# Attention's second pass: the masks come from ScalarE and VectorE copies instead of TensorE products

## The reference

```python
DILATED_PATTERNS = ((128, 1), (512, 4), (2048, 16))
def _dilated_pattern(qh, kh, vh, window, dilation):
    ...
    s = jnp.einsum('brnikge,brnjke->brnkgij', qs, kk)
    delta = ATTN_BLOCK + qi - kj
    band = (delta >= 0) & (delta <= steps)
    s = jnp.where(mask[:, None, None], s, -jnp.inf)
    m = jnp.max(s, axis=-1)
    pexp = jnp.exp(s - m[..., None])
    l = jnp.sum(pexp, axis=-1)
    o = jnp.einsum('brnkgij,brnjke->brnikge', pexp, vv)
```

## Time and profile before

| | |
|---|---|
| median of 3 runs | 3047.01 us |
| lowest, highest | 3043.47, 3048.12 us |
| profiled execution, span | 3041.8 us |
| profiled execution, its own device time | not given apart from the span |
| mixers phase in the trace | about 690 to 1223 us |
| second passes in the trace | 775.3 to 868.5, 913.7 to 1005.4, 1043.7 to 1223.0 us |

### The profile page before, as it was taken

One profiled execution on the slowest core, in us unless ns is written; L12 is line 12 of the kernel. 1 busy time (PEld: TensorE's weight loads), 2 busy tenths in 40 slices (PEclk: granted clock), 3 DMA queues, 4 the chain that ended last, 5 costly groups with the idle time before them and its releaser, 6 DMA issues. The chain is left out here.

```text
span 3041.8 us, 38698 instructions
## 1 busy us (share of the span) xinstructions
PE 2929.7 (96%) x14818; PEld 2301.9 (76%) x14818; DVE 1999.7 (66%) x2492; ACT 1147.6 (38%) x1734; POOL 284.0 (9%) x278
## 2 busy tenths in 40 slices
PE   7999999997999999899999999899999999999999
PEld 5678887884657566688778888788888788877887
DVE  7334555117575755545698899889998786776743
ACT  5332121212434344311255544554444444444321
POOL 0000000003435443000001000000000000000000
PEclk9999999998999999999999999999999999999999
DMA  4452222237775764634322234525542666443632
GB/s 145 166 190 64 62 83 62 74 84 194 200 186 152 203 154 136 199 124 142 140 104 83 97 122 159 197 84 194 194 152 104 243 210 222 149 158 114 192 113 67
DMA packets 260088, 435.02 MB, mean 143 GB/s; under 512 B 44013, under 2 KB 128493, under 8 KB 252877
## 3 DMA queue, kind: packets, MB, share of 16 engines
q1 hardware_dynamic: 255534, 408.32, 42.8%
q0 software_dynamic: 4384, 24.41, 2.2%
HBM read 312.18 MB, written 120.00 MB: 142 GB/s over the span
## 5 line engine op out<-in xcount | busy, mean ns | idle before, releaser
L103 PE MATMUL up_banks<-up_x_hi,up_w_hi 128*128 128x512 f32 x1232 | 484.0, 393 | 23.4 <-DVE up_x_lo L2682 8.2
L104 PE MATMUL up_banks<-up_x_lo,up_w_hi 128*128 128x512 f32 x1232 | 482.0, 391 | 0.0
L105 PE MATMUL up_banks<-up_x_hi,up_w_lo 128*128 128x512 f32 x1232 | 481.8, 391 | 0.0
L103 PE MATMUL inp_ps<-inp_h_hi,carry_q 128*128 128x512 f32 x896 | 353.1, 394 | 15.1 <-DVE inp_h_lo L202 9.7
L105 PE MATMUL inp_ps<-inp_h_hi,carry_k_two 128*128 128x512 f32 x896 | 349.8, 390 | 0.0
L104 PE MATMUL inp_ps<-inp_h_lo,carry_q 128*128 128x512 f32 x896 | 349.7, 390 | 0.0
L103 PEld LDWEIGHTS up_banks<-up_x_hi,up_w_hi 128*128 128x128 f32 x1232 | 232.8, 189 | 78.9 <-issue 15.7
L105 PEld LDWEIGHTS up_banks<-up_x_hi,up_w_lo 128*128 128x128 f32 x1232 | 232.8, 189 | 48.5
L104 PEld LDWEIGHTS up_banks<-up_x_lo,up_w_hi 128*128 128x128 f32 x1232 | 233.0, 189 | 48.2 <-issue 0.2
L2723 DVE SCALAR_TENSOR_TENSOR carry_rows<-carry_squares,up_conv_w,carry_rows 128x1024 f32<-128x1024 f32 x176 | 232.2, 1319 | 24.4 <-ACT carry_rows L2554 19.4
L103 PE MATMUL down_banks<-down_x_hi,down_w_hi 128*128 128x512 f32 x616 | 240.6, 391 | 7.1 <-DVE down_x_lo L2194 7.1
(11 more groups left out here) (378 smaller groups left out, 5366.2 us busy)
## 6 DMA issues: line engine op xcount, KB each, us to landing
carry_room<-in_w_up_dram SPq DMA_DIRECT2D x84, 512.0 KB, 4.4
act<-carry_rows SPq DMA_DIRECT2D x44, 512.0 KB, 2.9
carry_room<-cum_rows SPq DMA_DIRECT2D x16, 1024.0 KB, 6.6
carry_room<-x SPq DMA_DIRECT2D x7, 2048.0 KB, 9.4
carry_room<-in_w_in_dram SPq DMA_DIRECT2D x26, 512.0 KB, 5.9
xbc<-carry_room SPq DMA_DIRECT2D x12, 1024.0 KB, 5.7
carry_room<-xbc SPq DMA_DIRECT2D x16, 768.0 KB, 4.4
down_x<-act SPq DMA_DIRECT2D x12, 1024.0 KB, 7.2
```

The source lines that it names most:

```text
L103: pe.matmul(out, w_hi, x_hi, start=first, stop=False, skip_group_check=onto)
L104: pe.matmul(out, w_hi, x_lo, start=False, stop=False, skip_group_check=onto)
L105: return pe.matmul(out, w_lo, x_hi, start=False, stop=last, skip_group_check=onto)
```

## The change

Steps 0 and 1 of each second pass stay. For steps 2 to 39 the mask product is gone. ACT copies the mask of step k + 2 into the bank right after the exponential of an even step k (`lay_mask`, in `scalar`); DVE copies the masks of odd steps in a generator of its own (`lay_odd_masks`), due at k - 1.35. Both wait for the exponential of step g - 2. PE waits for the copy (`laid`) instead of the exponential, and all its products of that step run with start=False onto what the copy has left. 19 steps of each group are ACT's, 19 are DVE's: 76 copies for each engine. The pace changes too: a second pass is 69.0 long instead of 75.0, and a chunk of the scan comes every 23.1 instead of 24.5.

```diff
--- before.py
+++ after.py
@@ -788,6 +788,7 @@
          self.den_in, self.den_add, self.den_inv, self.inv_st) = (
             ph.sem(f"a_{n}") for n in ("built ones neg_in mm max m_mm m_out m_in m_s m_neg s_mm exp pv_mm "
                                        "o_add o_st den_in den_add den_inv inv_st").split())
+        self.laid = [ph.sem(f"a_laid_{engine}") for engine in ("act", "dve")]
         self.first_in = [ph.sem(f"a_first_in{n}") for n in range(2)]
         self.half_in, self.cleared = ph.sem("a_half_in"), ph.sem("a_cleared")
         self.k_in, self.k_last_in, self.q_in = ([ph.sem(f"a_{name}_in{n}") for n in range(len(self.SPANS))]
@@ -839,6 +840,31 @@
         if k < 2 * TT:
             return 1, k - TT, k % 4 < 3
         return 2, 2 * (k - 2 * TT), False
+
+    LAID = (STEPS - 2) // 2
+
+    def own_mask(self, g, k):
+
+        bank = self.banks[:, g % 2].rearrange("p (h b t) -> p h b t", h=2, b=2)
+        p, col, follows = self.step(k)
+        if p == 2:
+            return self.banks[:, g % 2], self.up_k[:, :, :].rearrange("p u t -> p (u t)")
+        if p == 1:
+            blocks = 2 if follows else 1
+            return bank[:, :, 0:blocks], self.both_k[:, :, 0:blocks]
+        if follows:
+            return (bank.rearrange("p h b t -> p h (b t)").rearrange("p h (i x) -> p h i x", i=RES),
+                    self.near_k[:, :, :, :, :].rearrange("p h i b m -> p h i (b m)"))
+        return bank[:, :, 0].rearrange("p h (i x) -> p h i x", i=RES), self.near_k[:, :, :, 0]
+
+    def lay_mask(self, engine, r, k):
+
+        g = r * self.STEPS + k
+        out, mask = self.own_mask(g, k)
+        if g == 2:
+            engine.wait_ge(self.built, 13)
+        engine.wait_ge(self.exp_s, g - 1)
+        return out, mask
 
     def readers(self, g):
 
@@ -1013,6 +1039,9 @@
                 bank = self.banks[:, g % 2].rearrange("p (h b t) -> p h b t", h=2, b=2)
                 blocks = slice(0, 2 if follows or k >= 2 * TT else 1)
                 act.activation(self.probs[:, g % self.RING, :, blocks], bank[:, :, blocks], ACT.Exp).then_inc(self.exp_s, 1)
+                if k % 2 == 0 and k + 2 < self.STEPS:
+                    out, mask = self.lay_mask(act, r, k + 2)
+                    act.activation(out, mask, ACT.Copy).then_inc(self.laid[0], 1)
 
     def vector(self, dve):
         yield self.at(1, 0, -0.5)
@@ -1040,6 +1069,13 @@
             if (which, r) == (1, 0):
                 yield self.at(1, 0, 0.9995)
                 self.turned(dve, 0)
+
+    def lay_odd_masks(self, dve):
+        for r in range(KVH):
+            for k in range(3, self.STEPS, 2):
+                yield self.in_step(r, k - 1.35)
+                out, mask = self.lay_mask(dve, r, k)
+                dve.tensor_copy(out, mask).then_inc(self.laid[1], 1)
 
     def largest(self, dve, r, s):
         g = r * self.FIRST + s
@@ -1226,35 +1262,35 @@
             pe.wait_ge(self.neg_in, 16 * (r + 1))
             pe.wait_ge(self.ones_s, 1 if r < KVH - 1 else 2)
             pe.wait_ge(self.a_max, self.FIRST * min(r + 2, KVH))
-        if g >= 2:
+        if g >= 2 and k < 2:
             pe.wait_ge(self.exp_s, g - 1)
         bank = self.banks[:, g % 2].rearrange("p (h b t) -> p h b t", h=2, b=2)
+        out, mask = self.own_mask(g, k)
+        if k < 2:
+            pe.matmul(out, self.ident_b[:, :], mask, start=True, stop=False)
+        else:
+            pe.wait_ge(self.laid[k % 2], self.LAID * r + k // 2)
         if p < 2:
             blocks, own = 2 if follows else 1, self.run(p, col, 1)
-            out, mask = bank[:, :, 0:blocks], self.both_k[:, :, 0:blocks]
             parts = [(out, col, blocks)]
-            if p == 0 and follows:
-                out = bank.rearrange("p h b t -> p h (b t)").rearrange("p h (i x) -> p h i x", i=RES)
-                mask = self.near_k[:, :, :, :, :].rearrange("p h i b m -> p h i (b m)")
+            if p == 0 and follows and col % RES == RES - 1:
                 half = P // RES
-                parts = ([(out, col, 2)] if col % RES < RES - 1
-                         else [(out[:, :, :, b * half:(b + 1) * half], col + b, 1) for b in range(2)])
-            elif p == 0:
-                out, mask = bank[:, :, 0].rearrange("p h (i x) -> p h i x", i=RES), self.near_k[:, :, :, 0]
-                parts = [(out, col, 1)]
-            pe.matmul(out, self.ident_b[:, :], mask, start=True, stop=False)
+                parts = [(out[:, :, :, b * half:(b + 1) * half], col + b, 1) for b in range(2)]
             for part, first, n in parts:
-                pe.matmul(part, k_two[:, own], self.queries(self.q_two[:, :, :], p, first, n), start=False, stop=False)
+                pe.matmul(part, k_two[:, own], self.queries(self.q_two[:, :, :], p, first, n), start=False, stop=False,
+                          skip_group_check=k >= 2)
             for part, first, n in parts:
-                last = pe.matmul(part, k_one[0:HD + 1, own], self.queries(self.q_max[:, :, :], p, first, n), start=False, stop=first + n == col + blocks)
+                last = pe.matmul(part, k_one[0:HD + 1, own], self.queries(self.q_max[:, :, :], p, first, n), start=False,
+                                 stop=first + n == col + blocks, skip_group_check=k >= 2)
             last.then_inc(self.s_mm, 1)
         else:
-            pe.matmul(self.banks[:, g % 2], self.ident_b[:, :], self.up_k[:, :, :].rearrange("p u t -> p (u t)"), start=True, stop=False)
             for i in range(2):
                 own = self.run(p, col + i, 1)
                 out = bank[:, :, i].rearrange("p h (c n) -> p h c n", c=NB)
-                pe.matmul(out, k_two[:, own], self.queries(self.q_two[:, :, :], p, col + i, 1), start=False, stop=False)
-                last = pe.matmul(out, k_one[0:HD + 1, own], self.queries(self.q_max[:, :, :], p, col + i, 1), start=False, stop=(i == 1))
+                pe.matmul(out, k_two[:, own], self.queries(self.q_two[:, :, :], p, col + i, 1), start=False, stop=False,
+                          skip_group_check=k >= 2)
+                last = pe.matmul(out, k_one[0:HD + 1, own], self.queries(self.q_max[:, :, :], p, col + i, 1), start=False,
+                                 stop=(i == 1), skip_group_check=k >= 2)
             last.then_inc(self.s_mm, 1)
 
     def values(self, pe, r, j):
@@ -1659,8 +1695,8 @@
         arena, e_arena = carry.room, carry.rows
         ident = ph.sb("ident", [P, P])
         made = ph.sem("made")
-        heads = Attention(ph, carry.out_last, carry.first_in, carry.q1, carry.k_two, *attention_given, ident, -27.0, (32.0, 75.0))
-        mixer = Ssd(ph, arena, e_arena, *ssd_given, ident, -5.0, 24.5, heads.end + 1.0)
+        heads = Attention(ph, carry.out_last, carry.first_in, carry.q1, carry.k_two, *attention_given, ident, -27.0, (32.0, 69.0))
+        mixer = Ssd(ph, arena, e_arena, *ssd_given, ident, -5.0, 23.1, heads.end + 1.0)
         block = ph.block()
 
         def begin_next(sp):
@@ -1702,7 +1738,7 @@
 
         @block.vector
         def _(dve):
-            weave(heads.vector(dve), heads.inverses(dve), mixer.vector(dve))
+            weave(heads.vector(dve), heads.lay_odd_masks(dve), heads.inverses(dve), mixer.vector(dve))
 
         @block.tensor
         def _(pe):
```

## The result

The changed kernel takes 3085.16 us (median of 4, 3078.68 to 3091.2) against 3045.24 us for the kernel before (4 runs). The ratio is 1.0135, 95% interval 1.0116 to 1.0154: **41 us slower**, where 10 us faster was forecast, and outside the range given (3018 to 3055). The profiled execution took 3085.39 us, its span is 3083.6 us.

The account below looks back on a forecast made before the run. PE was taken as the bound in second passes (busy 354.2 of 364.2 us). Saving -20, ACT copies +1, late DVE copies +9, pace 0 gave -10: 3031.8 + 5.2 = 3037 us, range 3018 to 3055.

Parts of the forecast that it names:

- PE's saving: Second passes: removing 152 mask products, less key weight loads laid bare behind narrow tiles, saves 20 us, between 9 and 33.
- no load covered: Case in which every weight load in second passes is laid bare without masks: only 9 us saved; chance 0.04.
- The copies' durations: Mask copies into the bank: 0.5 us each on ACT (0.6 in full), 0.69 on DVE, between 0.42 and 1.10.
- 0.9 for each burst, +9 us: DVE's late odd-step copies: 20 of 76 steps start too soon, in 10 bursts, +9 us, bounds 0 and 24.
- +1 for ACT: ACT's even-step copies: three of 76 steps start too soon, by 0.9 us together; +1 us, between 0 and 6.
- The worked places: Two DVE copies timed on the earlier trace: group 0 step 3, 1.4 us late; group 2 step 7, 1.1 late.
- Wait moved ... 0 in the sum: PE's exponential wait moves to DVE and ACT; scan work queued behind costs 0, as PE waits 6.7 us for state.
- rival (d): DVE's queue becomes the bound in second passes, scan products wait: at 2.5 us per chunk, 10 slower, 3057; chance 0.22.
- (b): Second-pass copies on time in DVE's gaps (43% idle), loads mostly covered: -20 to -33 us, 3014 to 3027; chance 0.20.
- I price no loss: Clock in second passes: granted 1.00 before, also where PE was busy 34.7 of 38.3 us, so no loss counted.
- the prediction's own signs of being wrong: Copies of 1.1 us, waits for DVE over 20 us, or a clock under 1.00 in a second pass.
- Pace: 0, between -3 and +4: New pace fixes only queue order; all queues shift, DMAs keep their semaphores: 0 us, between -3 and +4.

Follow-up runs that it names:

- e13: Changed kernel at the old pace (75.0 and 24.5), ACT copying all masks from step 2 on and DVE none: 3063.58 us, 1.0055 to the kernel before.
- e12: Changed kernel at the old pace (75.0 and 24.5), DVE's copies due at k - 0.9 instead of k - 1.35: 3059.48 us, 1.0042 to the kernel before.
- e15: Kernel before, masks on PE, with the new pace (69.0 and 23.1) and 76 DVE waits for exponentials, each with a two-element clear: 3064.80 us, 1.0065.
- e14: Changed kernel with the pace 69.0 and 23.2 instead of 69.0 and 23.1: 3079.37 us, 1.0121 to the kernel before.
- e1: Changed kernel with all copies kept but the old pace (75.0 and 24.5): 3065.66 us, 1.0059 to the kernel before.

## Why the prediction was wrong

**PE's saving was nearly right.** Forecast 20 us between 9 and 33; measured 17.7 less busy time without masks. A step behind a full-array product came down to the 0.46 us forecast: in the timeline after, two successive last-factor products (L1283) stand 0.47 apart, where the three products of a step took 0.70 in the earlier trace rows:

```profile
796.30 0.40 PE L1283 MATMUL mix_a_banks<-mix_q_max,mix_k_one 65*128 65x512 f32 x1
796.54 0.39 PE L1280 MATMUL mix_a_banks<-mix_q_two,carry_k_two 128*128 128x512 f32 x1
796.77 0.39 PE L1283 MATMUL mix_a_banks<-mix_q_max,mix_k_one 65*128 65x512 f32 x1
```

Behind narrow tiles the bare weight load kept most of the time. From the last narrow product to the last factor of the step the medians in the kernel without masks are 0.54 us in the first pattern (0.66 before, so 0.12 saved against 0.13 forecast) and 0.66 in the second (0.67 before, 0.01 against 0.02). What was mis-sized is the second pattern behind the scan's products on the full array: there the step of 512 columns went from 0.58 to 0.47, 0.11 saved where 0.23 was forecast. With no load covered the saving would have been 9 us. The sentence of the Trainium skill (TensorE: Matmul & The Clock Gate, Part 3) that a load overlaps running products only on another row group says so; the 0.47 contradicts it, as two loads of 0.19 to 0.20 and two products of 0.23 don't fit into it one after another. The same part also lets a load into the background weight buffer be pulled ahead, and the trace is in keeping with that.

**The copies' durations were right.** DVE's take 0.69 us as taken from the earlier trace rows, ACT's 0.60, where I wrote 0.5 back to back and 0.6 in full:

```profile
L1044 ACT ACTIVATE mix_a_banks<-mix_both_k 128x512 f32<-128x512 bf16 x32 | 19.3, 602 | 1.0
...
L1078 DVE CAST mix_a_banks<-mix_near_k 128x512 f32<-128x512 bf16 x24 | 16.6, 693 | 47.6 <-ACT mix_probs L1041 47.6
```

There was no double rate for the 16-bit operand: 128x256 takes 0.42, 128x512 0.69. The Trainium skill (VectorE: DVE Perf Modes, Why PSUM operands drop a tier) gives double rate only as the most next to PSUM, and single rate for fp32; the bank is fp32, and the measured single rate agrees. The some 3 us that I had by the first half of that rule did not come.

**The late masks were undersized.** "0.9 for each burst, +9 us", and +1 for ACT. PE's direct waits for masks were 17.1 (14 times) and 3.2 us. The worked places were of the right size (1.1 to 1.4 us; the longest now is 2.8), but I counted the bursts on the trace of before, in which PE reaches a step later than it would.

**"Wait moved ... 0 in the sum" is the first step that failed.** The group above says how long DVE stands before the copies of one mask alone, 47.6 us; over all it is

```profile
DVE mix_a_banks L1078 <- ACT mix_probs L1041: 102.6, 62, 14.8
```

Not all of that is lost, since DVE was idle for 156 of the 347 us before. I had named what queues behind it (the scan's xdt, decay products and state) and took PE's 6.7 us of waiting for the state as proof of cover. It was not: 76 waits alone cost 10 us, and in the changed kernel PE waits 14.6 us for the state (6.3 before) and 4.3 for `xdt` (0.4). That was rival (d), with its place and mechanism right, given 0.22 and a price of 2.5 us per chunk, 30 in all; at the old pace 35 were lost. But (d) is not the whole of it: with all copies on ACT, 17 us were lost without one copy on DVE. (Its counterweight in (b), 43% of DVE idle, is 44% by the earlier trace rows.)

**"I price no loss" for the clock is the second.** I argued from one first pass at 1.00 with PE busy 34.7 of 38.3 us (91%), and from the mean over a pass. The mean does not decide: the last second pass of the changed kernel had PE busy 83.9 of 89.6 us (94%) at a clock of 0.96. PE's pauses come bunched, about once a chunk, and behind such a pause the clock is granted at the lower level. That is 21 us in this profile, beside 30 us of idle time. It is no fixed price per pause: 22 us of idle time went with 20 of clock in e13, 25 with 10 in e12. A clock under 1.00 in a second pass, and waits for DVE over 20 us (17.1 + 14.6 + 4.3), were the prediction's own signs of being wrong.

**"Pace: 0, between -3 and +4" is the third.** It cost 12 alone. I wrote that all queues shift and that each DMA keeps its semaphore, and did not compute the due times pairwise, where 307.3 against 308.0 was to be read off the diff. The gap of 7 us is explained by it; the rest is not: the second passes are 8 us longer (355 against 347), more idle time and lower clock, from a cause that stays open.

**The sum.** In the terms of the prediction, by the profiles: saving -17 (forecast -20), late masks +20 (+10), less the 3 us of waits for exponentials that they replace, moved wait +12 (0), clock +21 (0), gap +8 (0); together 41. These are shares of one execution, not costs tried one by one. By the runs: removal -17, all else of the copies at the old pace +35 (together the measured 18), pace 12, which makes 30 of 41 us. The 11 that copies and pace cost together are not attributed, and with intervals of some 6, 4 and 6 us on the three figures they are known to about 9. Waits alone add up with the pace (e15); SyncE's order gave 4 us back in e14, which the intervals don't tell from nothing; and (1 - clock) x length nearly adds up, 13.7 us in e1 and 4.5 with the pace alone against 20.9 in the change.

## What to carry to other kernels

When a wait moves from the bound engine to another engine with an in-order queue, price it by what stands behind it there, not by that engine's busy share: 70 us of added work were free, 76 waits cost 10. To take a product off the tensor engine is worth its time less that of the weight load which it covered (17 us for 152 products here, 33 by the sum with all loads covered), and every pause that the hand-over adds can be paid again by a lower clock right behind it. When pace or due times change, compare the due times of pieces from different generators in pairs, for each engine; a flip by 0.7 units put two of the scan's loads before those that the next stage needed.

None of the versions tried beats the kernel before; the most that taking the masks off PE gave, in the run that leaves them out, is 17 us.

## What was not expected of the hardware

The clock varies where nothing was changed. From the first mask product to the first second pass the instructions of e1, e12 and e13 have the same pace and the same work, yet these stretches took 88.0, 82.0 and 81.8 us, and (1 - clock) x length in them was 18.8, 10.2 and 10.2 us. A single profile therefore splits a difference by stage only to within some 6 us, and medians of many runs are needed for 10.

Two halves that each cost nothing (ACT's even copies and ACT's odd copies, 0.9999 both) cost 17 us together on the same engine. The profiles say how. Each half paid its saving back: of the second passes' 347 us, PE's busy time less the clock's share fell by 6 and 9 us, while idle time rose by 4 and 6 and the clock took 3 and 5. Together the saving is 18, but idle time rose by 16.5 and the clock took 20. Why the clock took more than the two halves' 8 is not shown; single profiles scatter by up to 10 us in this.
